# A new order of steps in the mixing part of a hybrid decoder, and other quarter sums handed to DMA

## The reference

```
x += 1/2 * SwiGLU_a(RMSNorm(x))
h = RMSNorm(x);  P = h @ W_in        # ret q|k|v|gate, swa q|k|v, mem q, three branch gates
A: chunkwise retention, 4 heads, rotated q and k     (rq, rk, rv, rg)
B: sliding-window attention, 16 q heads / 2 kv heads (sq, skv)
C: attention into 256 memory tokens, 4 heads         (mk, mv, mq)
y = sum_b sigmoid(gate_b) * (branch_b @ W_up_b);  x += y @ W_o
x += 1/2 * SwiGLU_b(RMSNorm(x))
```

## Time and profile before

| | |
|---|---|
| median of 3 runs | 1461.79 us (1461.72 to 1462.51) |
| the profiled execution | 1461.72 us, span 1459.9 us |
| TensorE busy | 1437.9 us, 98% of the span |
| VectorE busy | 1141.4 us, 78% |
| ScalarE busy | 965.0 us, 66% |
| GpSimd busy | 109.9 us, 8% |
| mean granted clock of TensorE | 0.995 |
| DMA | 338.27 MB, 232 GB/s |

### The profile page before, as it was taken

How to read it: one execution, slowest core, us unless ns; L and a number is a source line. 1 busy time by engine, 2 the same in 40 slices (tenths; PEclk the granted TensorE clock), 3 DMA queues, 4 the chain that set the end, 5 groups by cost and what they waited for, 6 DMA issues and landing times.

```text
span 1459.9 us, 17935 instructions
## 1 busy us (share of the span) xinstructions
PE 1437.9 (98%) x6838; PEld 1192.9 (82%) x6838; DVE 1141.4 (78%) x1268; ACT 965.0 (66%) x1416; POOL 109.9 (8%) x123
## 2 busy tenths in 40 slices
PE   8999999999999999999999999999999999999997
PEld 5888888888888888888888888888888888888886
DVE  6998756899768468798789986569976875688984
ACT  6777666678756447676577775657776663576673
POOL 0000000051000000001000000000600000010000
PEclk9999999999999999999999999999999999999999
DMA  9899646574848377889839987556666655778881
GB/s 367 261 276 276 244 160 260 180 224 156 279 130 301 127 265 269 244 267 297 317 120 291 294 222 283 200 179 213 187 195 222 177 244 189 297 203 270 276 264 44
DMA packets 49092, 338.27 MB, mean 232 GB/s; under 512 B 5520, under 2 KB 6160, under 8 KB 8816
## 3 DMA queue, kind: packets, MB, share of 16 engines
q1 hardware_dynamic: 37392, 259.54, 46.8%
q0 software_dynamic: 8336, 59.64, 20.8%
q10 hardware_dynamic: 3280, 17.95, 3.2%
HBM read 329.77 MB, written 7.34 MB: 231 GB/s over the span
## 4 chain that ended last, share of the span: by engine, by line
PE 88%; DVE 5%; DMA 3%; ACT 2%; SPq 1%; issue 1%; POOLq 0%; POOL 0%; DVEq 0%; ACTq 0%
PE bank L761 27%; PE bank L763 27%; PE bank L762 27%; PE bank L818 4%; DVE w_lo L1563 3%; DMA raw<-in_stream 2%; DMA raw_q<-in_stream 1%; ACT w_hi L1169 1%; PE bank L1096 1%; PE bank L1078 1%; PE bank L995 1%; PE bank L969 1%; ACT prob L1469 0%; PE bank L981 0%; SPq L622 0%
## 5 line engine op out<-in xcount | busy, mean ns | idle before, releaser
L1563 DVE TENSOR_TENSOR w_lo<-raw,w_hi 128x1024 fp32r<-128x1024 f32 x352 | 425.9, 1253 | 177.4 <-ACT w_hi L1169 176.7
L1169 ACT ACTIVATE w_hi<-raw 128x1024 fp32r<-128x1024 f32 x352 | 352.3, 1053 | 199.4 <-PE bank L763 164.8
L761 PE MATMUL bank<-w_hi,hT_lo 128*128 128x512 f32 (+1 forms) x716 | 279.3, 390 | 0.3 <-issue 0.2
L763 PE MATMUL bank<-w_lo,hT_hi 128*128 128x512 f32 (+1 forms) x716 | 275.7, 385 | 0.0
L762 PE MATMUL bank<-w_hi,hT_hi 128*128 128x512 f32 (+1 forms) x716 | 275.4, 385 | 0.0
L761 PEld LDWEIGHTS bank<-w_hi,hT_lo 128*128 128x128 f32 x716 | 134.5, 188 | 29.0 <-issue 3.1
L763 PEld LDWEIGHTS bank<-w_lo,hT_hi 128*128 128x128 f32 x716 | 134.5, 188 | 27.1
L762 PEld LDWEIGHTS bank<-w_hi,hT_hi 128*128 128x128 f32 x716 | 134.7, 188 | 25.6
L761 PE MATMUL bank<-w_hi,S_lo 128*128 128x512 f32 x340 | 136.0, 400 | 0.9 <-ACT snap L1250 0.7
L763 PE MATMUL bank<-w_lo,S_hi 128*128 128x512 f32 x340 | 132.8, 391 | 0.0
L762 PE MATMUL bank<-w_hi,S_hi 128*128 128x512 f32 x340 | 132.4, 389 | 0.0
(11 more groups left out here) (229 smaller groups left out, 2466.0 us busy)
## 6 DMA issues: line engine op xcount, KB each, us to landing
raw<-in_stream SPq DMA_DIRECT2D x160, 1024.0 KB, 6.4
raw_b<-in_stream SPq DMA_DIRECT2D x33, 1024.0 KB, 7.4
raw_q<-in_stream SPq DMA_DIRECT2D x33, 1024.0 KB, 9.1
raw<-in_stream POOLq DMA_DIRECT2D x26, 1024.0 KB, 8.9
raw_x<-in_stream SPq DMA_DIRECT2D x18, 1024.0 KB, 4.9
raw_b<-in_stream POOLq DMA_DIRECT2D x15, 1024.0 KB, 9.7
raw_q<-in_stream POOLq DMA_DIRECT2D x11, 1024.0 KB, 12.0
raw_x<-in_stream POOLq DMA_DIRECT2D x4, 1024.0 KB, 10.2
```

The lines of the kernel that those rows point to most:

```text
L761: nc.tensor.matmul(dst, xl, wh[:, a:b], start=first, stop=False, skip_group_check=more)
L763: return nc.tensor.matmul(dst, xh, wl[:, a:b], start=False, stop=last, skip_group_check=more)
L1169: nc.scalar.activation(slots(o)[0][:, part], raw_slot(s)[:, part], ACT.Copy).then_inc(hi_split, 1)
L1563: nc.vector.tensor_tensor(lo[:, part], raw_slot(s)[:, part], hi[:, part].bitcast(F32), ALU.subtract)\
```

## The change

The list `SCHEDULE` is put in another order, and `ADDED` names other sums. The functions are unchanged.

```
--- before.py
+++ after.py
@@ -74,7 +74,7 @@
 MIX_PAIRS = {"sq": ("sq0", "sq1"), "rk": ("rq0", "rk0"), "rv": ("rv0", "rv1"), "rg": ("rg0", "rg1"),
              "gs": ("gs0", "gs1"), "mq": ("mq0", "mq1"), "gr": ("gr0", "gr1"), "gm": ("gm0", "gm1")}
 SCHEDULE = """
-mk0.1+xt0 mk1.0+xt1 sq0.0 S_sum mk1.1 skv.0 S_hi S_lo mkt sq1.0 sq1.1 sq0.1 skt mv0.0 sqt rk:5 mv0.1 s0 mv1.0 s1 e0 rk:1 rk:3 pt0 rk:6 mv1.1 rv0.0 mv_out pv0 rk:7 s2 e1 rk:2 rk:4 pt1 rg:5 rg:1 e2 pv1 rg:3 rv0.1 s3 rv1.0 pt2 rot rg:6 rv1.1 pv2 rqt e3 rg:7 rg:2 rkt mq1.0 rg:4 pt3 gs:5 rs gs:3 gs:1 pv3 gs:6 gs:2 st mq1.1 gs:7 us0.0 gs:4 ro us1.0 us0.1 re us1.1 mq0.0 mq0.1 gr:1 mqt gr:5 rt gr:3 gr:6 mkT_in gm0.0 mv_in gr:7 gr:2 gr:4 ms me mn ur0.0 ur0.1 mpt gm0.1 ur1.0 ur1.1 mpv um0.0 um1.0 um0.1 x_in gm1.0 mg0 gm1.1 um1.1 wo0.0 mg1 wo1.0 wo0.1 wo1.1+yt0
+mk0.1+xt0 mk1.0+xt1 mk1.1 skv.0 sq0.0 S_sum sq1.0 S_hi S_lo mkt sq1.1 sq0.1 skt mv0.0 sqt rk:5 mv0.1 s0 mv1.0 s1 e0 rk:1 rk:3 pt0 rk:6 mv1.1 mv_out rk:2 pv0 rk:7 e1 rv0.0 s2 rk:4 rg:5 rot pt1 rg:1 rqt pv1 rv0.1 e2 s3 rv1.0 e3 rg:3 pt2 rg:6 rv1.1 rkt rg:7 pv2 rg:2 rg:4 pt3 gs:5 rs gs:1 pv3 gs:3 gs:6 st gs:2 gs:7 us0.0 gs:4 ro us0.1 us1.0 mq1.0 us1.1 re mq1.1 mq0.0 mq0.1 gr:5 mqt gr:3 gr:1 rt mkT_in gr:6 gm0.0 gr:7 gr:2 gr:4 mv_in ms me ur0.0 mn x_in ur0.1 gm0.1 ur1.0 mpt gm1.0 ur1.1 mpv um0.0 um0.1 gm1.1 um1.0 mg0 um1.1 wo0.0 mg1 wo1.0 wo0.1 wo1.1+yt0
 """.split()
 
 PAIR_OF, STEPS = {}, []
@@ -117,7 +117,7 @@
 SUMS = {5: "11", 6: "22", 7: "12", 4: "21"}
 SUM_EARLY = {7: 1}
 LAST_USE = {"11": (5, 1), "12": (4,), "21": (2,), "22": (7,)}
-ADDED = {(0, 'gr'): (7, 4), (0, 'gs'): (7, 4), (0, 'rg'): (6, 7), (0, 'rk'): (7,), (1, 0): (7, 4), (1, 1): (6, 7, 4), (1, 2): (7, 4), (1, 3): (6, 7, 4), (2, 0): (6, 7, 4), (2, 1): (6, 7), (2, 2): (6, 7, 4), (2, 3): (6, 7, 4)}
+ADDED = {(0, 'gr'): (7,), (0, 'gs'): (7, 4), (0, 'rg'): (7, 4), (0, 'rk'): (6, 7, 4), (1, 0): (7, 4), (1, 1): (6, 7, 4), (1, 2): (7, 4), (1, 3): (6, 7, 4), (2, 0): (6, 7, 4), (2, 1): (6, 7), (2, 2): (6, 7, 4), (2, 3): (6, 7, 4)}
 
 
 def needs(l, pair, m):
```

## The result

| | before | after |
|---|---|---|
| median | 1462.15 us (4 runs, 1461.72 to 1463.78) | 1474.87 us (4 runs, 1473.60 to 1475.37) |
| the profiled execution | 1461.72 us, span 1459.9 | 1475.33 us, span 1473.5 |
| mean granted clock of TensorE | 0.995 | 0.992 |

The ratio is 1.0085, 95% interval 1.0068 to 1.0101: slower by 12.7 us. The forecast was 1469.0 us, with a range up to 1473.0; slower was right, and the size was not.

The account below looks back on a forecast made before the run. TensorE was taken as the bound, busy 1437.9 of 1459.9 us. From 1461.7 us, two `s3` stalls of 5.7 us, less 3.5 at `st` and 0.6 at `pt2`, gave 1469.0 us; whole range 1457.5 to 1473.

Parts of the forecast that it names:

- The waits at `st` and `pt2`: TensorE's waits in the mixing part, expected to go: -3.5 us at `st`, -0.6 us at `pt2` over two layers.
- The four signs: L969 waits some 5 us per layer; `stA` wait gone; rotations begin near 296 and 304; sum of 3.4 us ahead of `pv1`.
- The edits costed at nothing: Changed quarter sums, `gr` 4 as a VectorE sum, and units moved by a place or two: 0, moves bounded 0 to 1 us.
- The rival of a second new wait: `pv3` waits for the bank of the first `rs`: 1 to 2.5 us per layer on top, 1471 to 1474; chance 0.12.
- `s3`: Scores step waits for `pv1`'s bank, freed late by VectorE slowed beside GpSimd's rotation: 5.7 us in each layer.
- the Trainium skill's rule: VectorE with two SBUF inputs and GpSimd shut each other out for a whole instruction; this would make the `s3` stall 6.6 us.
- the sum: Whole-kernel total: 1461.7 + 2 x 5.7 for `s3` - 3.5 at `st` - 0.6 at `pt2` = 1469.0 us.
- my range for the stall: Wait before `s3`, 4 to 7 us in each layer, giving 1465.6 to 1471.6 us.

Follow-up runs that it names:

- 1: Kernel before's list and rk, rg sums up to `rkt`, changed kernel's list and gr sum behind it; 1465.62 us, ratio 1.0013 against the kernel before.
- 7: Front of the kernel before, back of the changed one, with `e3` moved from behind `rqt` to right behind `rg:6`; 1462.04 us, ratio 0.9993 against before.
- experiment 11: Kernel before with only `mq1.1` moved from ahead of `gs:7` to behind it; 1459.11 us, ratio 0.9971 against before.
- 12: Front of the kernel before, back of the changed one, with `mq1.0` kept behind `rkt` and `mq1.1` behind `gs:7`; 1457.68 us, ratio 0.9960 against before.
- Experiment 4: Changed kernel with the rotation's four GpSimd instructions cut to one column per head; 1457.99 us, ratio 0.9959 against the kernel before.
- 3: Changed kernel with the sum for `rg:6` made by an accumulating DMA instead of VectorE; 1467.51 us, ratio 1.0033 against the kernel before.
- 8: Changed kernel with `rg:3` put back right behind `pv1`; 1470.63 us, ratio 1.0046 against the kernel before.
- Experiment 5: Changed kernel with thirty matmuls of zeros into a free bank during TensorE's wait before `s3`; 1471.27 us, ratio 1.0052 against the kernel before.
- experiment 10: Kernel before with the first half of the split of `rv1.0` made four times on VectorE; 1478.52 us, ratio 1.0103 against before.
- experiment 9: Kernel before with the first half of the split of `rv1.0` made twice on VectorE; 1465.70 us, ratio 1.0017 against before.
- 2: Changed kernel's list and sums up to `rg:2`, kernel before's list behind it from `mq1.0`; 1479.10 us, ratio 1.0100 against the kernel before.
- 6: Changed kernel with `rot` back behind `pt2` and `rqt` back behind `rv1.1`; 1484.37 us, ratio 1.0135 against the kernel before.

## Why the prediction was right in its sign and wrong in its size

**The waits at `st` and `pt2`: right.** -3.5 us at `st`, by the traces of after and of experiments 1, 7, 11 and 12; experiment 11 shows the cause with one step moved. The four signs that I had named for being right all came: the wait at L969 in each layer, the one at L818 gone, rotations from 294.8 and 304.3, and a sum of 3.37 us ahead of `pv1`. The 0.3 us per layer at `pt2` are inside `rv1.0`'s net figures.

**The edits costed at nothing: nearly right.** The sum for `rg` 5 waited for a landing till 291.45 (forecast 290.20), and the split behind it took 3.48 us beside the first rotation, so `pv0`'s bank was late: 0.75 us in layer 0. That slowing I had counted only from `rg:5`'s split on. The rival of a second new wait, priced at 1 to 2.5 us per layer, was 0.5 and 0.2 us at `gs:1`.

**`s3`: mechanism right, the size 0.9 us per layer short.** Forecast and trace agree step by step in layer 0: splits of `rv0.1` and `rv1.0` done at 318.2 against 316.4, sum at 321.7 against 319.7, split of `rg:3` at 324.0 against 323.0, bank free at 325.1 against 325.5. Two errors nearly cancel. The four splits took 7.91 us beside the rotation and not 9.4; but the rotations ended at 324.2 and not at 321.0, so the split of `rg:3` took 3.41 us and not 2.3, and an instruction of 128x8 took 1.22 and not 0.16 (my 1.1 us from the first small instruction to the freed bank is its time without a rotation). Forecast 2 x 5.7 = 11.4; measured 6.4 + 6.8 = 13.2, inside the 4 to 7 us that I gave each. By the Trainium skill's rule (SBUF — State Buffer, Who interferes with whom) I had worked out 6.6, which came nearer than my own sum, but by luck: it rests on a sum slowed by up to 2.1 us, and the sum took 3.37 us and not 2.29, 1.1 us more. Experiment 4 shows that the slowing is the cause, 3 that the sum and the place of the rotation make 2.6 us of it, 8 that the order of TensorE's steps only shifts how much is covered.

**The step that failed: the sum.** It counted a wait of TensorE at its own length. With the stall as measured it would have given 1461.7 + 13.2 - 3.5 - 0.6 = 1470.8, inside the range. It had no term for the clock behind the wait, which measured 2 x 1.35 in `s3` and 1.3 + 0.5 in `rv1.0` (the net 1.0 and 0.2 with `pt2`'s 0.3 put back), 4.5 us; with it the sum is 1475.3, and the profiled execution took 1475.33. That it meets so closely is luck, since `s2` and `gs:1` (1.4 us more in the trace) and `pt1` and the FFNs (1.6 us less) are left out of it. Experiment 5 takes this term away and leaves the wait; experiment 10 makes it in the kernel before. Both edges of my range for the stall had the same hole, so no stall within that range could have mended it: its upper end, 7 us, gave 1471.6.

The term was there to be read in the trace of before. The 4.3 us wait in the first FFN, which I had put aside as not edited, is followed there by matmuls that start 0.42 us apart and not 0.227, and the clock's record has 6.83 us at 0.50:

```profile
37.27 0.80 PE L761 MATMUL bank<-w_hi,gT_lo 128*128 128x512 f32 x1 [4.34 <-DVE gT_lo L1581]
37.87 0.63 PE L762 MATMUL bank<-w_hi,gT_hi 128*128 128x512 f32 x1
38.29 0.63 PE L763 MATMUL bank<-w_lo,gT_hi 128*128 128x512 f32 x1
```

**What stays open.** Why the wait in layer 1 is 0.4 us longer than in layer 0; TensorE had already waited 0.75 us before `s2` in layer 0 and not in layer 1, and so came to `s3` less early there, but no run tests it. Where experiments 11 and 12 get what they gain beyond their traced waits. And what decides how long the low clock lasts: its length does not follow the wait alone, as the last section shows.

## What to carry to other kernels

When TensorE is the bound, a wait of some us that an edit puts before it can cost more than its length: look in the trace of the kernel before for the granted clock behind waits of that size, wherever they stand, and add what the next matmuls lose at half speed. When two engines slow each other, the stretch of overlap is itself stretched; work it out for both, to the end of the slower one, and include the small instructions. And when a step with a long run on GpSimd is moved, list what stands on GpSimd's queue on both sides of it: DMAs that wait there for a split decide when it starts.

## What the runs showed of the hardware

How long TensorE stood still before `s3`, and how long the record of the granted clock then shows 0.50: 1.0 us, no fall (experiment 9); 3.4 and 3.8 us, 3.41 us each (8); 5.4 us twice, 6.83 us (10); 6.3 and 6.7 us, 6.83 us (after); 6.8 and 6.1 us, 10.24 and 6.83 us (2). At `rqt`, 11.3 us gave 13.65 us (6), and a wait of only 2.1 us among transposes and matmuls of 64 columns gave 10.24 us (3). Other waits do not fall in line with these: before `st` of layer 1, 3.6 us with no fall (9) and 2.7 us with 3.41 us at 0.50 (10); before `pt3`, 2.6 us in each layer with 3.41 us in layer 1 and none in layer 0 (1); in the first FFN, 4.3 us with 6.83 us (before) and 4.5 us with 3.41 us (after). So the same wait can have different prices. Matmuls of zeros whose result nobody reads kept the clock at 1.00 through 6.5 and 6.7 us of delay (5).

Beside the rotation, the 128x8 instruction at L1816 takes 0.70 to 1.22 us and not 0.16: it waits out the GpSimd instruction that runs. Its end lies 0.02 to 0.03 us behind that one's: 319.59 behind 319.56 and 1036.50 behind 1036.48 in the kernel before, 297.76 behind 297.74, 324.25 behind 324.22 and 1049.77 behind 1049.75 after the change.
